# Two block attentions on one core: outputs scaled one step later, dense tiles among the attention's steps, and a conv norm that takes both spans at once

## What is computed

```
def conv_branch(u_glu, u_gate, conv_w, conv_b, ln_g, ln_b, w_proj):
    a = u_glu[..., :D_CONV] * jax.nn.sigmoid(u_glu[..., D_CONV:])
    a = depthwise_conv(a, conv_w, conv_b)
    a = jax.nn.silu(layer_norm_2(a, ln_g, ln_b))
    return (a * jax.nn.silu(u_gate)) @ w_proj
...
def merge_branches(a_glu, a_gate, o_na, n_gate, o_wa, w_gate, merge,
                   conv_w, conv_b, cln_g, cln_b, w_proj_a, w_proj_b, w_proj_c, w_o):
    y_a = conv_branch(a_glu, a_gate, conv_w, conv_b, cln_g, cln_b, w_proj_a)
    y_b = (o_na * jax.nn.silu(n_gate)) @ w_proj_b
    y_c = (o_wa * jax.nn.silu(w_gate)) @ w_proj_c
    g_a, g_b, g_c = jnp.split(merge, 3, axis=-1)
    y = jax.nn.sigmoid(g_a) * y_a + jax.nn.sigmoid(g_b) * y_b + jax.nn.sigmoid(g_c) * y_c
    return y @ w_o
```

## Time and profile before

| what | us |
|---|---|
| median of three runs | 4264.07 |
| lowest and highest | 4256.93, 4265.66 |
| profiled execution | 4263.09 |
| its span | 4261.9 |
| PE busy in the span | 3820.0 (90%) |
| DVE busy | 2266.1 (53%) |
| ACT busy | 1473.6 (35%) |
| POOL busy | 1207.1 (28%) |

### The profile page before, as it was taken

How to read it: one execution, slowest core, us unless ns; L and a number is a source line. 1 busy time by engine, 2 the same in 40 slices (tenths; PEclk the granted TensorE clock), 3 DMA queues, 4 the chain that set the end, 5 groups by cost and what they waited for, 6 DMA issues and landing times.

```text
span 4261.9 us, 54184 instructions
## 1 busy us (share of the span) xinstructions
PE 3820.0 (90%) x21364; PEld 3163.2 (74%) x21364; DVE 2266.1 (53%) x3704; ACT 1473.6 (35%) x2514; POOL 1207.1 (28%) x793
## 2 busy tenths in 40 slices
PE   5999768889999999798999698789998989789989
PEld 4888646778888888657888586568876867568767
DVE  6556683566556777646433688621144239730442
ACT  3223423444224323344323322342234222342352
POOL 1112434233014201304201424613211334514314
PEclk8999989999999999899999898899999989999999
DMA  7564214235554555203333211002110212102202
GB/s 262 173 200 146 97 63 157 104 124 172 179 182 139 186 184 164 97 34 114 120 99 97 89 60 44 27 26 70 45 50 11 69 41 79 53 21 101 70 23 92
DMA packets 131595, 433.12 MB, mean 102 GB/s; under 512 B 14480, under 2 KB 14480, under 8 KB 130704
## 3 DMA queue, kind: packets, MB, share of 16 engines
q1 hardware_dynamic: 130912, 427.04, 29.8%
q10 hardware_dynamic: 432, 2.62, 0.2%
HBM read 427.51 MB, written 2.10 MB: 101 GB/s over the span
## 4 chain that ended last, share of the span: by engine, by line
PE 66%; DVE 19%; ACT 6%; issue 5%; POOL 2%; DMA 1%; SPq 0%; DVEq 0%; ACTq 0%; POOLq 0%
PE ps L595 19%; PE ps L596 19%; PE ps L597 19%; DVE cut L2016 5%; ACT cut L1751 2%; DVE cut L1144 1%; PE ps L621 1%; PE ps L622 1%; ACT cut L1760 1%; PE ps L623 1%; PE ps L1628 1%; POOL cut L524 1%; DVE cut L1776 1%; DVE cut L1782 1%; DVE cut L996 1%
## 5 line engine op out<-in xcount | busy, mean ns | idle before, releaser
L595 PE MATMUL ps<-cut 128*128 128x512 f32 (+1 forms) x5216 | 1874.6, 359 | 182.3 <-POOL cut L524 43.0
L596 PE MATMUL ps<-cut 128*128 128x512 f32 (+1 forms) x5216 | 1834.3, 352 | 0.0
L597 PE MATMUL ps<-cut 128*128 128x512 f32 (+1 forms) x5216 | 1832.4, 351 | 0.0
L595 PEld LDWEIGHTS ps<-cut 128*128 128x128 f32 x5216 | 1012.7, 194 | 343.5 <-issue 116.4
L524 POOL TENSOR_TENSOR cut<-cut 128x1024 fp32r<-128x1024 f32 (+3 forms) x334 | 735.8, 2205 | 1379.8 <-ACT cut L514 1379.1
L596 PEld LDWEIGHTS ps<-cut 128*128 128x128 f32 x5216 | 1014.0, 194 | 131.2 <-issue 6.3
L597 PEld LDWEIGHTS ps<-cut 128*128 128x128 f32 x5216 | 1011.7, 194 | 125.6
L514 ACT ACTIVATE cut<-cut 128x1024 fp32r<-128x1024 f32 (+3 forms) x680 | 630.9, 936 | 596.0 <-PE ps L597 476.2
L524 DVE TENSOR_TENSOR cut<-cut 128x1024 fp32r<-128x1024 f32 (+2 forms) x346 | 421.3, 1220 | 445.5 <-ACT cut L514 445.5
L842 POOL TENSOR_TENSOR cut<-cut 128x512 fp32r<-128x512 f32 (+1 forms) x100 | 137.0, 1370 | 1014.4 <-ACT cut L802 1014.4
L2016 DVE SCALAR_TENSOR_TENSOR cut<-cut,cols 128x512 f32<-128x512 f32 (+1 forms) x330 | 279.9, 848 | 11.7
(11 more groups left out here) (283 smaller groups left out, 3851.5 us busy)
## 6 DMA issues: line engine op xcount, KB each, us to landing
cut<-in_ffn_in SPq DMA_DIRECT2D x200, 512.0 KB, 4.0
cut<-in_mod_w SPq DMA_DIRECT2D x128, 512.0 KB, 4.2
cut<-in_ffn_out SPq DMA_DIRECT2D x96, 384.0 KB, 3.1
cut<-in_ffn_out SPq DMA_DIRECT2D x96, 320.0 KB, 3.0
cut<-in_w_ada SPq DMA_DIRECT2D x48, 512.0 KB, 3.5
cut<-in_w_merge SPq DMA_DIRECT2D x48, 512.0 KB, 3.5
cut<-in_even_in SPq DMA_DIRECT2D x36, 512.0 KB, 3.5
cut<-in_proj SPq DMA_DIRECT2D x48, 256.0 KB, 2.6
```

The source lines that it names most:

```text
L595: te.matmul(o, hi[:, k - ka, w], xs[0], start=k == 0, stop=False)
L596: te.matmul(o, hi[:, k - ka, w], xs[1], start=False, stop=False)
L597: ins = te.matmul(o, lo[:, k - ka, w], xs[0], start=False, stop=last)
```

## The change

Five things change, all in the second network. VectorE multiplies the output of job i-4 at step i, not of job i-3. The attentions take a table of work to be done in a step (`at_step`): three of the six tiles of nv's second half, two agate tiles, or the last three of merge and proj, and two wgate tiles. Of the other three nv tiles, two stand ahead of nk's head scale and one behind it. The pairs run in the order of MERGES, in which proj m-1 follows merge m. The conv norm makes both spans' means, then both spans' squares, with temporaries of their own, and one set of square roots and reciprocals, with agate tiles 2 and 3 between. ScalarE's split of Y waits for merge 7 and each Y, not for the last matmul of proj 7.

```diff
         last, n = self.first(m) + len(self.cuts) - 1, self.first(m)
+        edge = n if self.name[0] == "nv" and self.name[2] == 1 else last
 
         def room(i):
             plain = i >= NRAW and not SLABS[i - NRAW].lin.split and i - NRAW >= last
-            return not plain and (SLABS[i].before is None or SLABS[i].before < last)
+            return not plain and (SLABS[i].before is None or SLABS[i].before < edge)
...
+MERGES = [("merge", 0)] + [x for m in range(1, 8) for x in (("merge", m), ("proj", m - 1))] + [("proj", 7)]
...
+    def pe_tok_tiles(name, x, until, ts, ncol=256):
+
         L = LIN[name]
-        for m in range(L.groups):
+        for t in ts:
+            b = bank[name, t, 0] = yield from pe_take(until(t))
+            for i, (n, ka, kb) in enumerate(L.parts(0)):
+                if t == 0:
+                    yield from pe_weights(n)
+                hi, lo = [tiles(n, v) for v in halves(n)]
+                for k in range(ka, kb):
+                    xs = x(k, t)
+                    te.matmul(PS[b][:, 0:ncol], xs[0], hi[:, k - ka, :], start=k == 0, stop=False)
+                    te.matmul(PS[b][:, 0:ncol], xs[0], lo[:, k - ka, :], start=False, stop=False)
+                    ins = te.matmul(PS[b][:, 0:ncol], xs[1], hi[:, k - ka, :], start=False, stop=k == L.kt - 1)
+                if kb == L.kt:
+                    ins.then_inc(*sig("p_mm", name, t, 0))
+                elif t == L.toks - 1:
+                    ins.then_inc(*sig("p_mm", name, "part", i))
+        if ts[-1] == L.toks - 1:
+            at[("p_mm", name, "end")] = newest["p"]
...
-    def pe_pairs(tag, jobs):
+    def pe_pairs(tag, jobs, mid):
         n = len(jobs)
         for i in range(n + 3):
             if i < n:
                 J, w = jobs[i], jobs[i]["w"]
+                for key in J["ready"]:
+                    te.wait_ge(*(yield key))
...
+            yield from mid(i)
...
+                if i - 2 < len(clear):
+                    se.wait_ge(*(yield clear[i - 2]))
...
+    def dve_pairs(tag, jobs, mid, clear=()):
         n = len(jobs)
-        for i in range(n + 3):
+        for i in range(n + 4):
...
+                if i - 2 < len(clear):
+                    ve.wait_ge(*(yield clear[i - 2]))
...
-            if 0 <= i - 3 < n:
-                o = jobs[i - 3]["out"]
-                ve.wait_ge(*(yield "a_av", tag, i - 3))
-                ve.tensor_tensor(o, o, PS[bank["p_pv", tag, i - 3]][:, 128:256], ALU.mult).then_inc(*sig("v_o", tag, i - 3))
-            yield from between(i)
+            if i >= 4:
+                o = jobs[i - 4]["out"]
+                ve.wait_ge(*(yield "a_av", tag, i - 4))
+                ve.tensor_tensor(o, o, PS[bank["p_pv", tag, i - 4]][:, 128:256], ALU.mult).then_inc(*sig("v_o", tag, i - 4))
+            yield from mid(i)
...
-    def pe_conv_norm(l):
+    def conv_tmp(h0, i, n):
+
+        return t512[(8 if h0 else 0) + i][:, 0:n]
+
+    def pe_conv_means(l):
         for c0, n, h0, g in spans(l):
             b = bank["p_cm", l, h0] = yield from pe_take(("a_cm", l, h0))
...
+    def pe_conv_squares(l):
+        for c0, n, h0, g in spans(l):
             b = bank["p_cv", l, h0] = yield from pe_take(("a_cvs", l, h0))
             for t in range(4):
                 te.wait_ge(*(yield "a_csq", l, h0, t))
-                te.matmul(PS[b][:, 0:n], ones, t512[t % 2][:, 0:n], start=t == 0, stop=t == 3).then_inc(*sig("p_cv", l, h0, t))
-
-    def act_conv_norm(l):
+                te.matmul(PS[b][:, 0:n], ones, conv_tmp(h0, t % 2, n), start=t == 0, stop=t == 3).then_inc(*sig("p_cv", l, h0, t))
+
...
+    def act_conv_squares(l):
         for c0, n, h0, g in spans(l):
             se.wait_ge(*(yield "p_cm", l, h0))
-            if h0:
-                se.wait_ge(*(yield "v_cn2", l, 0, 3))
-            se.activation(t512[3][:, 0:n], PS[bank["p_cm", l, h0]][:, 0:n], ACT.Copy, scale=2.0).then_inc(*sig("a_cm", l, h0))
+            se.activation(conv_tmp(h0, 3, n), PS[bank["p_cm", l, h0]][:, 0:n], ACT.Copy, scale=2.0).then_inc(*sig("a_cm", l, h0))
+        for c0, n, h0, g in spans(l):
...
-                se.activation(t512[t % 2][:, 0:n], AG[:, t, h0:h0 + n], ACT.Square).then_inc(*sig("a_csq", l, h0, t))
+                se.activation(conv_tmp(h0, t % 2, n), AG[:, t, h0:h0 + n], ACT.Square).then_inc(*sig("a_csq", l, h0, t))
+
+    def act_conv_norm(l):
+        for c0, n, h0, g in spans(l):
             se.wait_ge(*(yield "p_cv", l, h0, 3))
-            se.activation(t512[2][:, 0:n], PS[bank["p_cv", l, h0]][:, 0:n], ACT.Sqrt, bias=epsc(EPS), scale=2.0).then_inc(*sig("a_cvs", l, h0))
-            for t in range(4):
+            se.activation(conv_tmp(h0, 2, n), PS[bank["p_cv", l, h0]][:, 0:n], ACT.Sqrt, bias=epsc(EPS), scale=2.0).then_inc(*sig("a_cvs", l, h0))
+        for t in range(4):
+            for c0, n, h0, g in spans(l):
                 o = AG[:, t, h0:h0 + n]
...
+        for c0, n, h0, g in spans(l):
+            r = conv_tmp(h0, 2, n)
             ve.wait_ge(*(yield "a_cvs", l, h0))
-            ve.reciprocal(t512[2][:, 0:n], t512[2][:, 0:n]).then_inc(*sig("v_cr", l, h0))
-            ve.wait_ge(*prev("v"))
-            for t in range(4):
+            ve.reciprocal(r, r).then_inc(*sig("v_cr", l, h0))
+        for t in range(4):
+            for c0, n, h0, g in spans(l):
                 o = AG[:, t, h0:h0 + n]
                 if t == 0:
+                    ve.wait_ge(*(yield "v_cr", l, h0))
                     ve.wait_ge(*(yield "a_csq", l, h0, 3))
-                ve.tensor_tensor(o, o, t512[2][:, 0:n], ALU.mult).then_inc(*sig("v_cn2", l, h0, t))
+                ve.tensor_tensor(o, o, conv_tmp(h0, 2, n), ALU.mult).then_inc(*sig("v_cn2", l, h0, t))
...
+    def pe_merge(l, i, groups, ready, items=MERGES, beside=nothing):
+        for kind, m in items:
+            name = (kind, l, i, m)
+            if kind == "merge":
+                yield from pe_linear(name, nrhs, groups, lambda _, gi: ("a_sg", l, i, m, gi), none)
+            else:
+                yield from pe_linear(name, brhs, groups, lambda _, gi: ("v_y0", l, i, m, gi), ready if m == 0 else none)
+                yield from beside(m)
...
+    def pool_merge(l, i, items=MERGES):
+        for kind, m in items:
+            yield from pool_linear((kind, l, i, m), nothing)
+
+    def at_step(table):
+
+        return lambda i: table[i]() if i in table else nothing(i)
...
+                                ready=[("v_hn", ("nk", l), t, 1)] if qb == 0 else [],
+                                vready=[("a_nv", l, t // 2, 5)] if qb == 0 and t % 2 == 0 else [],
...
-        yield from pe_linear_tok(("nv", l, 1), nlhs, lambda t, c0: ("a_nv", l, 1, t), none)
+
+        def nv1(*ts):
+            return pe_tok_tiles(("nv", l, 1), nlhs, lambda t: ("a_nv", l, 1, t), ts)
+
+        def agate(m):
+            return pe_linear(("agate", l), nrhs, QG, lambda m, gi: ("a_ag", l, m, gi), none, ms=[m])
+
+        yield from nv1(0, 1)
         yield from pe_head_scale(("nk", l), GR, 6)
-        te.wait_ge(*(yield "v_hn", ("nk", l), 3, 1))
-        te.wait_ge(*(yield "a_nv", l, 1, 5))
-        yield from pe_pairs(("na", l), na_jobs(l))
-        yield from pe_linear(("agate", l), nrhs, QG, lambda m, gi: ("a_ag", l, m, gi), none)
-        yield from pe_conv_norm(l)
-        yield from pe_merge(l, 0, range(NT), QG, lambda k, gi: [(("v_bl0", "g_bl0")[k % 2], l, k)])
+        yield from nv1(2)
+        n = len(na_jobs(l))
+        yield from pe_pairs(("na", l), na_jobs(l), at_step({
+            0: lambda: nv1(3), 1: lambda: nv1(4), 2: lambda: nv1(5), n: lambda: agate(0), n + 1: lambda: agate(1)}))
+        yield from pe_conv_means(l)
+        yield from agate(2)
+        yield from pe_conv_squares(l)
+        yield from agate(3)
+        yield from pe_merge(l, 0, QG, lambda k, gi: [(("v_bl0", "g_bl0")[k % 2], l, k)])
...
+        def beside(m):
+            if m == 0:
+                yield from pe_head_scale(("wq", l), QG, 0)
+            if m in (1, 2):
+                yield from pe_wk_norm(l, m - 1)
+            if m == 3:
+                yield from pe_rope((l, 4), WK[:, 0, 0:512], ("v_wn", l, 0), 512, con("rax"))
+            if m in (2, 3, 4, 5):
+                yield from pe_rope((l, m - 2), WQ[:, m - 2, 0:512], ("v_hn", ("wq", l), m - 2, 0), 512, con("rax"))
+
+        def merge(items):
+            return pe_merge(l, 1, QG, lambda k, gi: [("g_bl", "ngate", l, k, gi)], items, beside)
+
+        def wgate(m):
+            return pe_linear(("wgate", l), nrhs, QG, lambda m, gi: ("a_gate", "wgate", l, m, gi), none, ms=[m])
+
+        yield from merge(MERGES[:-3])
         te.wait_ge(*(yield "v_rp", (l, 4)))
-        te.wait_ge(*(yield "a_wv", l, 5))
-        yield from pe_pairs(("wa", l), wa_jobs(l))
-        yield from pe_linear(("wgate", l), nrhs, QG, lambda m, gi: ("a_gate", "wgate", l, m, gi), none)
-        yield from pe_merge(l, 2, range(NT), QG, lambda k, gi: [("g_bl", "wgate", l, k, gi)])
-        close("p", ("merged", l))
```

(33 more changed lines are left out.)

155 lines of the change are left out of this document (67 added, 88 removed).

## The result

The changed kernel takes 4234.26 us (median of four runs, 4232.26 to 4240.29) against 4264.43 us (median of four, 4256.93 to 4265.66); the ratio is 0.9935, with a 95% interval of 0.9918 to 0.9952. That is faster, by 30 us, less than half of the 67 that I had forecast, and outside the range. The span is 4232.4 us, 29.5 shorter.

A forecast was written before the change was run, and what follows sets the result against it. PE (TensorE, 66% of the chain) was taken to bound the kernel, gains lying where it waits. Terms of 48.5 us (l=0) and 18.7 (l=1) summed to 67.2, so 4196.9 us from a median of 4264.07; range 4178 to 4217.

The forecast's parts named there:

- First attention, start: Head of each first attention: everything from the head scale on comes four tiles earlier, 12.0 us (l=0) and 11.7 (l=1).
- Outputs one step later: All four attentions, later multiplication: waits on ScalarE's copies go, 38 PE waits of 1.05 us come; +21.5 us in all.
- I take the middle: New PE wait on VectorE, 38 × 1.05 us: between a loss of 40 us and 40 us more gain.
- the tap stretch: VectorE-bound 75.6 us with conv taps in an l=0 attention: loses 11.3 us of waits, bounds 0 and 13.8.
- Second attention, start: Head of each second attention: merge 7, proj 6 and 7 fill steps 0 to 2; 5.5 us (l=0), 5.9 (l=1).
- Conv norm: Stretch around the conv norm: squares' PE waits go under agate tiles 2 and 3; 4.2 us (l=0), 0.9 (l=1).
- a tail of 7.9 us: After the conv norm's last square sum in l=0: a chain of 24.7 us, of which merge 0 and 1 fill 16.8.
- Behind the last steps: Gate tiles after the attentions: PE waits 2.3 us for a bank that ScalarE's first silu frees; −1.0 (l=0), −1.3 (l=1).
- the waits of the last steps: Ends of the second attentions: block-copy waits filled by tiles, giving back 1.3 us (l=0) and 1.0 (l=1).
- First output tile: First output tile: earlier copies of Y leave only the last Y's chain; 5.0 us (l=0), 2.8 (l=1), bounds 0 and 10.
- Slower: Rival, chance 0.03: VectorE's lateness reaches PE 38 times through the bank wait; loss from 2.8 us a wait, 4275 at 3.1.
- Half gain: Rival, chance 0.17: fillers do not fit PE's holes or the conv tail eats the gain; 37 to 50 us, 4214 to 4227.

The follow-up runs named there:

- the put-back kernel: The changed kernel with VectorE's multiplication put back to job i-3 at the end of step i: 4232.27 us, ratio 0.9928.
- The experiment: The changed kernel with the multiplication behind VectorE's first maximum (4202.12 us), with the conv norm put back as it was: 4205.26 us, ratio 0.9861.
- the experiment: The changed kernel with the multiplication behind the first maximum (4202.12 us), with ScalarE's high and VectorE's low halves of Y made earlier: 4209.34 us, ratio 0.9869.

## Why the prediction was wrong

Of the 67 us 36 are missing: 25 in the four attentions (−16.7 in l=1, −8.3 in l=0) and 10 in the two rows that hold the output.

**First attention, start: right.** 12.1 and 12.0 us for 12.0 and 11.7, and the tiles between the steps cost next to nothing (the put-back kernel's first attentions take 152.7 and 102.0 us for 152.8 and 101.1).

**Outputs one step later: the step that failed.** It reads "VectorE takes it 0.04 us after the transposes", from which came 1.05 us of wait, and then "I take the middle because VectorE stands idle before that copy today". The row was right and the conclusion wrong. VectorE was idle before the copy because TensorE was late with the transposes; and TensorE was late because of the waits on ScalarE that the same sum took away. In the very step of the earlier trace rows its transposes had waited 2.09 us:

```profile
3701.80 0.63 PE L1719 MATMUL ps<-const,cut 128*128 128x128 f32 x4 [2.09 <-ACT cut L1760]
```

Without them TensorE ends its transposes while VectorE is still in the maxima, and the copy and the multiplication start when these are through. One step laid out would have shown it: from the start of the first score VectorE needs 1.25 us to begin and 3.18 for four maxima, the small operations, the copy and the multiplication, 4.4 us, while TensorE is through its scores and transposes after 3.0; that is a wait of 1.4 to 1.5, and measured are 1.46. In four l=1 jobs 4 × 0.41 us more makes the 23.1 into 24.7, which is the window's 24.67. In the second attention the wait is 20.1 us in 12, 1.67 each, and the same four jobs take 23.40 for my 20.8. Together with the tap stretch the term came to about 0 instead of +21.5. (The four parts of the 1.05, 0.04, 0.69, 0.29 and 0.07, add to 1.09; over 38 waits that is 1.5 us and changes nothing here.)

In l=0 the gain came, but smaller, and one of its two pieces fits only by luck. Six jobs of the first attention take 26.76 for 25.9, those of the second 23.64 for 24.4. In the second PE stands 3.0 us, not 2.1; the piece is shorter than forecast because PE busy fell to 20.61 at clock 1.00, where the sum had kept 22.31. The tap stretch and what follows gave 10.9 for 15.9.

**Second attention, start: right in l=0**, 5.1 us for 5.5, and short in l=1, 3.6 for 5.9. The stretch ahead of the first score took 78.2 us there in every kernel with the new order, so the 2.3 that are missing are no noise; which part of the sum they belong to stays open.

**Conv norm: the waits right in l=0, the gain smaller.** The experiment gives some 2.2 us for 4.2 in l=0, and in l=1 nothing that is told from noise for 0.9. The square sums don't wait, and where the sum had a tail of 7.9 us and 2.1 of hi/lo wait, 10.0 together, the profile has the 9.7. PE's idle time in the stretch of l=0 fell from 17.9 to 15.3 us, 2.6 of the 6.6 that the row gains; the rest is PE's busy time, and no run says why. In l=1 PE waits 2.3 and 8.8 us behind the attention, 11.1 together, where it had waited 10.6 before and the sum had 9.7.

**Behind the last steps: the waits right.** Four of 2.3 us. Of the drain that the Trainium skill's page "ScalarE: Activation LUTs", "What ACT_TABLE_LOAD costs", states (some 1380 ns more at each switch), nothing shows here either: ScalarE loads at 2784.77 for 1.28 us and is in the silu at 2786.07.

```profile
2784.48 0.28 ACT L1799 ACTIVATE cut<-ps 128x128 f32<-128x128 f32 x1 [0.38 <-PE ps L1773]
2784.77 1.28 ACT L2351 ACT_TABLE_LOAD   x1
2786.07 0.87 ACT L2351 ACTIVATE cut<-ps 128x512 f32<-128x512 f32 x2
```

But I had set "the waits of the last steps" against it, and nothing shows that they were given back: the put-back kernel's second attentions, with the tiles taken off, take 105.7 and 79.7 us for 103.2 and 79.9. The last stretch of l=1 loses 3.5 us: the new wait of 2.3, an output tile that gains nothing, and 1.2 that no wait shows.

**First output tile: the second step that failed.** I had counted the chain of the last Y as what decides. What decides is the first one: TensorE waits for the low half of Y 0, and that stands on VectorE behind all additions, those of proj 7 too. The wait was 6.4 and is 6.6 us, 3.6 and 3.6 in l=1. The sum had 7.8 us there; the tile of l=0 is 0.95 us shorter. Nor would moving VectorE's low halves alone have given them, since GpSimd's come next, as the experiment shows.

**The rivals.** "Slower" named the right mechanism, the bank wait, and put its price only at a catastrophe of 2.8 us, with 0.03. "Half gain" gave 4214 to 4227 by another way, fillers that don't fit, which isn't what happened: by one execution of the put-back kernel they cost 3.1 us. What I lacked was the case between: the bank wait at 1.5 us, which eats the whole term.

## To carry to other kernels

When an edit removes a wait of engine A, don't keep the idle times of B that the trace shows beside it: lay out one step with A's work alone, B's work alone and every hand-over between them, and take the longest loop. For an operation that frees a buffer for another engine, ask for both ends: when its input is ready, and when the other engine needs the buffer; its place in the queue is between the two. Here moving one 0.28 us operation of each step four or five instructions forward was worth 43 to 45 us, more than all the rest of the change (33). And at the head of a stage, ask for the first operand that is needed, not for the last one that is made.
